# TensorE's four loops written out as a straight program in a hybrid pool, convolution and attention decoder step

## What is computed

```python
xn = rms_norm(x, norm1_g)
proj = xn @ w_in
u_pool, h_b, h_c, h_x, q, k, v, f_logit = jnp.split(proj, [o1, o2, o3, o4, o5, o6, o7], axis=-1)
...
y_att = attn_fn(q, k, v, logf)
...
mix = jnp.concatenate([rms_norm(y_pool, g_pool), rms_norm(y_conv, g_conv), rms_norm(y_att, g_att)], axis=-1)
x = x + mix @ w_o
xn2 = rms_norm(x, norm2_g)
a, gate = jnp.split(xn2 @ w_up, 2, axis=-1)
a_conv, ffn_state = causal_dwconv(a, prev_ffn, ffn_conv_w)
x = x + (jax.nn.silu(a_conv + ffn_conv_b) * gate) @ w_down
```

## Time and profile before

| | |
|---|---|
| median of three runs | 3076.17 us |
| lowest and highest | 3073.31, 3076.94 us |
| span of the profiled execution | 3079.8 us |
| TensorE matmuls busy | 2865.3 us, 93% of the span, 19952 instructions |
| TensorE weight loads busy | 2414.7 us, 78% |
| VectorE busy | 1492.1 us, 48% |
| ScalarE busy | 744.4 us, 24% |
| instructions fetched (queues q8 and q14) | 2.56 MB and 0.79 MB |

### The profile page before, as it was taken

One profiled execution on the slowest core, in us unless ns is written; L12 is line 12 of the kernel. 1 busy time (PEld: TensorE's weight loads), 2 busy tenths in 40 slices (PEclk: granted clock), 3 DMA queues, 4 the chain that ended last, 5 costly groups with the idle time before them and its releaser, 6 DMA issues.

```text
span 3079.8 us, 54057 instructions
## 1 busy us (share of the span) xinstructions
PE 2865.3 (93%) x19952; PEld 2414.7 (78%) x19952; DVE 1492.1 (48%) x5784; ACT 744.4 (24%) x968; POOL 18.1 (1%) x57
## 2 busy tenths in 40 slices
PE   6967999999999977699899999999999999999998
PEld 4954546545546324599899999999999999999998
DVE  6367566566566357633543434343434334343433
ACT  5211101101101136622422222222222222222221
POOL 1000000000000000000000000000000000000000
PEclk8978999999999987899999999999999999999999
DMA  6468898898898853233122222222232223222221
GB/s 215 134 232 316 311 381 328 321 383 331 321 376 329 312 177 108 67 97 128 64 93 91 92 83 83 96 97 83 83 103 90 83 83 110 84 83 83 102 90 59
DMA packets 265873, 516.23 MB, mean 168 GB/s; under 512 B 14162, under 2 KB 171435, under 8 KB 265076
## 3 DMA queue, kind: packets, MB, share of 16 engines
q1 hardware_dynamic: 257828, 496.26, 45.4%
q10 hardware_dynamic: 5760, 10.49, 0.9%
q0 software_dynamic: 2032, 6.13, 0.5%
HBM read 489.24 MB, written 24.02 MB: 167 GB/s over the span
## 4 chain that ended last, share of the span: by engine, by line
PE 58%; DVE 2%; issue 2%; ACT 1%; DVEq 0%; ACTq 0%
PE ps L624 57%; DVE t_work L1333 1%; PE ps L627 1%; DVE t_rmax L1650 0%; DVE t_aux L1333 0%; DVE t_aux L1590 0%; ACT t_aux L1196 0%; ACT t_aux L1198 0%; ACT L1196 0%; DVE t_work L1598 0%; ACT t_wh L1021 0%; ACT L1061 0%; DVE t_wl L1333 0%; DVE t_work L342 0%; ACT t_work L1226 0%
## 5 line engine op out<-in xcount | busy, mean ns | idle before, releaser
L624 PE MATMUL ps<-t_xh,t_wh 128*128 128x260 f32 x4608 | 951.2, 288 | 44.0 <-issue 25.0
L624 PE MATMUL ps<-t_xh,t_wl 128*128 128x260 f32 x4608 | 939.3, 286 | 0.0
L624 PE MATMUL ps<-t_xl,t_wh 128*128 128x260 f32 x4608 | 938.8, 286 | 0.0
L1333 DVE TENSOR_TENSOR t_wl<-t_wraw,t_wh 128x1024 fp32r<-128x1024 f32 x376 | 459.7, 1224 | 882.9 <-ACT t_wh L1021 882.8
L1021 ACT ACTIVATE t_wh<-t_wraw 128x1024 fp32r<-128x1024 f32 x376 | 398.1, 1060 | 1926.3 <-PE ps L624 1925.0
L624 PEld LDWEIGHTS ps<-t_xh,t_wh 128*128 128x128 f32 x4608 | 722.4, 192 | 85.3 <-issue 65.9
L624 PEld LDWEIGHTS ps<-t_xl,t_wh 128*128 128x128 f32 x4608 | 721.6, 192 | 8.0 <-issue 8.0
L624 PEld LDWEIGHTS ps<-t_xh,t_wl 128*128 128x128 f32 x4608 | 722.2, 191 | 0.0
L1459 DVE CUSTOM_DVE_ANT_0 t_work<-t_r,t_work 128x128 f32<-128x128 f32 x2048 | 455.8, 287 | 225.2 <-DMA t_r<-in_cache_k 214.8
L624 PE MATMUL ps<-t_r,t_pr 128*8 128x512 f32 x1024 | 455.9, 592 | 33.0 <-DMA t_r<-in_cache_v 31.4
L624 PEld LDWEIGHTS ps<-t_r,t_pr 128*8 128x8 f32 x1024 | 83.7, 89 | 359.4 <-issue 270.7
(11 more groups left out here) (186 smaller groups left out, 1082.4 us busy)
## 6 DMA issues: line engine op xcount, KB each, us to landing
t_r<-in_cache_k SPq DMA_DIRECT2D x256, 512.0 KB, 7.0
t_r<-in_cache_v SPq DMA_DIRECT2D x256, 512.0 KB, 6.3
t_wraw<-in_w_up SPq DMA_DIRECT2D x44, 2048.0 KB, 9.0
t_wraw<-in_w_down SPq DMA_DIRECT2D x22, 2048.0 KB, 8.0
t_wraw<-in_w_in SPq DMA_DIRECT2D x20, 2048.0 KB, 9.0
t_wraw<-in_w_o SPq DMA_DIRECT2D x8, 2048.0 KB, 10.4
scr_proj<-t_stg ACTq DMA_DIRECT2D x40, 256.0 KB, 5.0
t_aux<-scr_proj SPq DMA_DIRECT2D x12, 768.0 KB, 4.7
```

What stands on the lines that cost most here:

```text
L624: return pe.matmul(out, lhsT, rhs, start=start, stop=stop)
L1333: return dve.tensor_tensor(out, in0, in1, op)
```

## The change

TensorE's four loops become plain Python loops: the program of each pass is written out, with constants in place of registers. The other engines' programs are the same as before, with their loops. TensorE's list of instructions has no REGISTER_ALU and no COMPARE_AND_BRANCH left.

```diff
-        def attention(eng, step_):
+        def attention(eng, step_, unrolled=False):
 
             step_(0, 0, 2)
             step_(1, 1, 2)
-            with eng.Fori(1, HEADS // 2 - 1) as j:
-                step_(j * 2, 0, 2)
-                step_(j * 2 + 1, 1, 2)
+            if unrolled:
+                for j in range(1, HEADS // 2 - 1):
+                    step_(j * 2, 0, 2)
+                    step_(j * 2 + 1, 1, 2)
+            else:
+                with eng.Fori(1, HEADS // 2 - 1) as j:
+                    step_(j * 2, 0, 2)
+                    step_(j * 2 + 1, 1, 2)
...
-            with pe.Fori(1, DEC - 1) as r:
+            for r in range(1, DEC - 1):
                 round_(r, True, True, True)
...
-            attention(pe, head_step)
+            attention(pe, head_step, True)
...
-            with pe.Fori(1, 4) as i:
+            for i in range(1, 4):
                 out_tiles(i, range(4))
...
-            with pe.Fori(0, GROUPS - 1) as i:
+            for i in range(GROUPS - 1):
                 up(i, 0, range(2, 10))
                 down(i, 20, T_FF // 2 + 5)
```

## The result

The changed kernel takes 3056.47 us (median of four runs, 3050.14 to 3058.29) against 3076.56 us before (3073.31 to 3079.37). The ratio is 0.9935, with a 95% interval of 0.9924 to 0.9947: 20 us faster, between 16 and 23. The forecast was 3037 us, with a range that ended at 3055, so the gain is half of the one foretold. The profiled execution is the fastest of the four: its span is 3048.4 us, 31.4 under that of before.

What follows compares the result with a forecast made beforehand. TensorE was taken to bound the ConvFFN groups, with jumps back costing 39.8 us (27.6 pauses, 12.2 slower clock); rounds, output projection and heads 0. So 3076.2 - 39.8 = 3036.4, rounded to 3037 us, range 3028 to 3055.

Steps and rivals of the forecast that it cites:

- The bound: ConvFFN groups: TensorE alone limits them; writing out the loop removes pauses and slow clock at nine seams, minus 39.8 us.
- Rival B: Groups' seams: the pause belongs to the hand-over between projections and appears again; no effect, 3076 us, chance 0.03.
- rival C: Groups' seams: VectorE's chain wait partly replaces the pauses, or low clock turns up elsewhere; gain 22, 3054 us, chance 0.08.
- Rounds: 0, between -5 and +2 us: Cache rounds: free jumps, and newly fetched instructions in rounds 2 to 6 cost nothing, judged by rounds 1 and 7.
- rival A: Rounds: fetching falls behind and late packets stop TensorE; about 25 new packets cost 112 us, giving 3149 us, chance 0.03.
- the same gain off the median: Whole kernel: the profiled execution's 39.8 us gain taken off the median, 3076.2 to 3036.4 us, rounded to 3037.
- The term of 12.2 us for the clock: Groups: part of the 39.8 us, TensorE's slower 1.2 GHz clock behind the seams' pauses, counted as regained.
- Rival D: Rounds' and output projection's loops: seven seams cost 4.4 us each, so 31 us more gain, 3006 us, chance 0.02.
- the rule in the prediction: Skill's rule: engines hold two blocks of 256 instructions, so rounds and output loops would stall too; sum 31 us larger; rejected.

Runs made afterwards that it cites:

- e1: Only TensorE's ConvFFN loop written out, against the kernel before: 3049.75 us against 3074.34, ratio 0.9922.
- e3: ConvFFN, output projection and heads written out on TensorE, rounds' loop kept, against the kernel before: 3046.91 us against 3074.34, ratio 0.9919.
- e9: Only TensorE's ConvFFN loop written out, run again, against the kernel before: 3047.95 us against 3077.35, ratio 0.9902.
- e4: The full change once more, against the kernel before on the same chip: 3051.66 us against 3074.34, ratio 0.9925.
- e11: The full change again, against the kernel before on another shared chip: 3051.04 us against 3077.35, ratio 0.9920.
- e2: Only TensorE's loop of rounds written out, against the kernel before: 3103.94 us against 3074.34, ratio 1.0094.
- e5: The kernel before, all loops kept, with 30 semaphore increments on TensorE ahead of the ConvFFN: 3060.64 us against 3079.04, ratio 0.9939.
- e6: Only the rounds written out, plus 10 semaphore increments ahead of the ConvFFN, against the kernel before: 3069.56 us against 3079.04, ratio 0.9964.
- e7: The kernel before, unchanged, for a second profile: 3075.27 us against 3079.04 in its other runs, ratio 0.9992.
- e8: ConvFFN alone written out, plus 8 extra DRAM-to-DRAM copies a round by ScalarE in rounds 1 to 6, against the kernel before: 3052.36 us against 3079.04, ratio 0.9912.

## Why the prediction was half right

**The bound, right.** The groups are TensorE's alone, and what the seams cost came back: nine periods of 138.37 us, where 138.2 to 138.6 was foretold, the clock at 1.00, 1245.3 us in all against 1244.2, an issue row of 3.4 us plus one of 0.8, 157 packets on q8 (155), 82 in nine groups (9 a group). Rival B falls with this, and rival C with it: no other wait took the seam's place, and the chain of VectorE and ScalarE kept up. C's number was close to the measured one, but not its mechanism.

**The first step that failed: "Rounds: 0, between -5 and +2 us".** It measured +8.3 us in the first profile, and 3069.56 - 3060.64 = 8.9 us in timed runs with equal seams. Rounds 1 and 7 of the kernel before, which fetched, were too few and too unlike to bound it: round 7 is shorter than the others with fetches as well (111.00 us in the changed kernel), so its 112.48 was no sign that packets are free. The mean of rounds 2 to 6 went from 113.5 to 115.1 us. Round 1, which fetches in both programs, took 113.97 and 115.79 us, so two rounds could not settle a question of 1.6 us. The step also had too few instructions: 1083 a round are 4.2 packets, not 3.7, and five rounds brought 21. The packets did not stop TensorE for its own program, as rival A had it: there is no issue wait in the rounds. Rival A named the right place and the wrong price. Pages landed later on the mean (6.46 against 6.30 us), and TensorE waited longer for value pages (23.5 against 18.1 us in rounds 2 to 6). But e1, e3 and e9 waited as long, 22 to 25 us, with no packet in these rounds. So what makes the rounds longer, the packets, the straight code or something third, is not shown.

**The second: "the same gain off the median".** For the profiled execution the forecast was 3040.0 us, and its span is 3048.4: of the 20 us that the forecast was off, 8.4 stand there, as much as the rounds took longer. The other 11.7 lie between the profile and the median. The forecast put the median 3.6 us under the span, and it is 8.1 us above it. The results give time and span of each execution, 1.7 us apart, so the one profiled before took some 3081.5 us, more than any of its four runs; the one profiled after was the fastest of its four. The groups are the same 1245.3 us in every profile of the full change, and the rounds are not: e4, with 812.6, took 3054.76 us, and e11, with 803.6, took 3048.53.

Part of it was to be seen before. The second profile has 1278.9 us in place of 1284.0: the pauses are alike (28.5 and 28.6 us in the issue rows), but the lower clock followed five seams in the one and three in the other. The term of 12.2 us for the clock was an upper draw; about 8 to 9 is the mean of two.

With both mended the sum is 36.2 - 8.9 = 27 us. The three comparisons of the full change give 20 (16 to 23), 23 (17 to 29) and 25 (20 to 29). That this is near is in part luck, since the two terms don't add up so. The 8.9 us were measured where the groups are a loop; where they are straight, the same step costs 1.9 and 3.1 us (e4 against e1, e11 against e9, by the medians). And the ConvFFN alone, with the rounds untouched, gains 24 and 30 us instead of 36. So 6 to 12 us are missing where straight rounds have no part. One lead: looped rounds took 4 to 8 us longer in the profiles of kernels whose groups are straight than in the others, with page landings alike (6.30 us) and 22 to 25 us instead of 18 to 20 us of TensorE's waits for value pages in rounds 2 to 6. TensorE's program is the same up to there. What a longer program changes (where things lie in DRAM, for instance) was not tried, and the cause stays open.

**Rival D, wrong as expected.** Heads and output projection gave nothing measurable (e3 against e1), and at the rounds' seams nothing was to be had.

**On the rule of the Trainium skill.** The Trainium skill, "Runtime: NRT & Kernel Launch", section "Instruction fetch mechanics", says that a taken branch whose target is not held forces a fetch before execution goes on. The groups' seams agree, with 2 us for it, and the blocks of 256 instructions that the section names fit the place of the second pause (e2, e5, e6). Its 2048 instructions for TensorE fit as well: a body of 1101 stayed, bodies of 2200 and 2343 did not. The two blocks of the rule in the prediction do not fit, since 1101 and 780 stayed.

## What to carry to other kernels

A loop whose body is longer than what the engine holds (here 2200 and 2343 instructions, not 1101) pays at each jump back, and the price depends on where its head lies in a block: look for "issue" waits at the loop's seam and for instruction packets in the DMA queue, and try a few padding instructions before unrolling. Unroll only the loops that show these waits; a loop that stays resident has free seams, and writing out this one cost 9 us beside looped groups and 2 to 3 beside straight ones. Count the body by what the trace records, not by the program's list. A change to one part moves all the code behind it, so a fall or rise in an untouched loop can be its new position. And a sum from one profile should be set against a second one where a part of it (here the clock and the rounds) comes and goes, and its execution's time against the median.

## What was not expected of the hardware

- A pause costs more than itself. Behind pauses of 2 us the lower clock (1.2 GHz) followed at two of nine seams, in e5 and in e6; in the loop of before and e7, whose two pauses add up to some 3.3 us, at five and at three of nine; in e2, at 4.1 to 4.8 us, at all nine. At one of those five and two of those three the clock was low from the first pause on, and the second pause did not come: the 13 matmuls then last 2.8 us instead of 1.6. In between, matmuls of 260 columns start 0.217 us apart instead of 0.120.
- Thirty instructions that do nothing are worth 19 us of 3079, by position alone.
- An instruction packet of 16 KB takes 1.0 us on its engine, beside 0.17 us for a 4 KB packet of a page. Twice the volume in 1 KB packets (e8) cost nothing measurable in the time.
- TensorE kept a loop of 1101 instructions with no packet on q8 for five rounds.
